# Ranking steps of the next expert head spread over two heads, and PSUM sums copied at once at a tile change

## The chip, the cores and the metric

One of the cores of a Trainium2 chip runs the whole program as one launch. Each core has five engines with queues of their own: PE (TensorE, matmuls into the accumulator memory PSUM), DVE (VectorE, elementwise work, reductions, top-8 searches), ACT (ScalarE, activation functions and copies), POOL (GpSimd, here the issuer of the indirect gathers) and SP (SyncE, here the issuer of plain transfers). 16 DMA engines move data between the large memory and SBUF. Engines meet through semaphores only. The metric is the device time of the program in microseconds, as the median of several runs. A difference of 0.2% of it is about the smallest that can be told from none.

## The reference

Two layers over 256 latent tokens (with a context of 256 tokens), model width 1024. Each layer is a mixer (a gated convolution with a gated DeltaNet in the first layer, multi-head latent attention in the second), followed by a channel mixer with product-key experts. The change touches the latter:

```python
def peer(h, w_q, sub_keys, u_tab, v_tab):      # P_BLOCK = 128 tokens, P_HEADS = 8, P_NKEYS = 128, P_TOPK = 16
    tok = h.reshape(-1, P_BLOCK, D)
    def one(hb):
        q = (hb @ w_q).reshape(P_BLOCK, P_HEADS, 2, P_DKEY // 2)
        s = jnp.einsum('thpk,hpnk->thpn', q, sub_keys).astype(jnp.float32)
        s1, i1 = lax.top_k(s[:, :, 0], P_TOPK)
        s2, i2 = lax.top_k(s[:, :, 1], P_TOPK)
        cand = (s1[..., :, None] + s2[..., None, :]).reshape(P_BLOCK, P_HEADS, P_TOPK * P_TOPK)
        sc, pos = lax.top_k(cand, P_TOPK)
        idx = (jnp.take_along_axis(i1, pos // P_TOPK, axis=-1) * P_NKEYS
               + jnp.take_along_axis(i2, pos % P_TOPK, axis=-1))
        gate = jax.nn.softmax(sc, axis=-1).astype(hb.dtype)
        act = jax.nn.gelu(jnp.einsum('td,thkd->thk', hb, u_tab[idx]), approximate=False)
        return jnp.einsum('thk,thkd->td', gate * act, v_tab[idx])
```

For each token and head two sets of 128 scores are cut to their 16 best, the 256 sums of pairs to the 16 best again, and those 16 experts' rows (a u row and a v row of 1024 numbers each) are fetched. The dot product of the token with u, through a gelu and times the gate, weighs v in the sum. The first layer does this for four tiles of 128 tokens (two of context, two of latents), the second for two.

## The kernel before

The program is a row of blocks; every engine has to reach the end of a block before any of them starts the next. The first block projects the inputs, runs the first layer's mixer for the context tiles (`mixer_dve(dve, 0)` and its fellows), and scores their experts. The second, `sums_and_mixer`, computes the expert sums of all four tiles of the first layer, 32 heads of a tile (G = 0 to 31), with the mixer of the other two tiles woven in. The third is the second layer's attention up to the scores. The last, `last_sums`, does the sums of two tiles (G = 32 to 47).

**One head.** A head has 16 experts per token, k = 0 to 15. POOL (`sums_pool`, L1255) gathers for each k one row pair per partition into one of eight ring slots of 8 KB per partition, as soon as `slot_free` tells that the slot is free again. DVE (`head_dve`, L1427) waits for the slot and forms the dot product of u with the tile's tokens. After every second k it tells ACT (`sums_act`), which computes gelu (L1270), the coefficient (L1271) and for each k a diagonal matrix of coefficients (L1275). PE (`head_pe`, L1342) multiplies diagonals and v rows, in a group of 16 matmuls of 64 rows and 512 columns for the two slots, adds them up in four PSUM banks, and frees both slots. So a head has eight pairs, j = 0 to 7.

**Sums.** Slots of a pair go to different halves of the partitions of PSUM: banks `sum_bank(i, c)` hold the sum of row half i of the tokens, once in the partitions of half i (the straight half) and once in those of the other (the crossed half). They are added at the end of a tile: ACT copies the crossed halves into the tile's place in `hx2` (`tile_sum_act`, L1311), DVE adds the straight ones to it (`tile_sum_dve`, L1317) and raises `peer_taken`. At the first head of the next tile PE waits for that (`tile_open_pe`, L1319) and clears all banks with 16 matmuls by zero (L1328); all the others add (`start=False`). Within a block DVE does this adding after its dot product k = `SUM_AT` = 3 of the next tile's first head.

**Ranking.** `rank_dve` is a generator of 16 steps, each ended by a wait for DVE's own instructions. It takes one head's 256 scores to expert numbers and gates: a copy of the scores (L1355), top-8 searches and replacements (L1360 to L1365) for both key sets, the 256 candidates (L1368), two rounds of top 8 among them (L1372 to L1381), positions split in two numbers (L1384, L1385), casts of uint32 to float32 (L1372, L1387), two one-hot masks times index tables and their reductions (L1390, L1394, L1398), then the expert numbers and gates (L1402 to L1406). While head G's dot products run, the ranking of head G+1 advances by two steps after each of k = 1 to 8 (`RANK_SLOTS`). ACT's exponential for its gates (`gate_exp_act`, L1281) is issued in the pair j = 2; it loads another activation table, and the next gelu loads its own again. The first head of a block has its ranking done in the block before it (`first_rank_dve`), between two copies of scores out of PSUM (L801 in the first layer, L1752 in the second).

**Mixer.** In `sums_and_mixer` each of ACT, PE and DVE calls `between()` at the pairs in `STAGE_AT` = (0, 4, 6), on DVE after k = 1, 9 and 13. A call runs the next stage of the mixer of the other two tiles, 46 stages in all, in the queue's order, waits included.

**Others.** `tile_start_dve` copies the tile's tokens to `hx_cur` (L1418). `peer_residual_dve` (L1461, L1464) multiplies a finished sum by its gate and adds it to the stream.

## Time and profile before

| | |
|---|---|
| Median of 3 runs | 2910.38 us (2910.12 to 2912.04) |
| The profiled execution | 2908.8 us |
| Its span, first to last instruction | 2907.0 us |
| Mean granted TensorE clock | 0.802 of full speed |
| Busy: PE, DVE, POOL, ACT | 1930.8, 1785.0, 971.5, 901.1 us |
| Mean rate of the DMA engines | 318 GB/s |

Each run's time is that of the whole program on the device; the span of the profile leaves out what lies before the first and after the last instruction. Busy times overlap, so they don't add up to the span. A row of a timeline gives the start in us, the duration in us, engine, line, operation, what it writes and reads, how many instructions are merged into the row, and in brackets how long the engine had been idle before, and what ended that idleness. `PEld` is PE's loading of weights, which runs beside its matmuls.

### The profile page before, as it was taken

How to read it: one execution, taken by the hardware profiler on the slowest of the kernel's cores; microseconds unless marked ns; L12 is line 12 of the kernel's file. 1: busy time of each engine (PE TensorE's matmuls, PEld its weight loads, DVE VectorE, ACT ScalarE, POOL GpSimd, SP SyncE). 2: the span in 40 equal slices, each digit the busy share in tenths (PEclk: the TensorE clock that was granted, in tenths of full speed). 3: DMA queues.
4: the chain of work that ended last, by engine and by line, in shares of the span. 5: the costliest groups of instructions: out<-in, count | busy, mean ns of one | idle time of the engine just before them, and what ended most of it. 6: DMA issues, size and time to landing. Idle time of an engine off the chain costs nothing. (4 is left out here: it accounts for less than half of the span.)

```text
span 2907.0 us, 31687 instructions
## 1 busy us (share of the span) xinstructions
PE 1930.8 (66%) x11320; PEld 836.7 (29%) x11320; DVE 1785.0 (61%) x4221; ACT 901.1 (31%) x2534; POOL 971.5 (33%) x897
## 2 busy tenths in 40 slices
PE   4999988666666666765555465566996555555564
PEld 2445885333332321331111111113455111111111
DVE  3044872787777774565777767764234677767774
ACT  1043111333333242332333333333221333333332
POOL 3000320344334432333444444450001444444542
PEclk7999998888778877886777777767998877777767
DMA  9112862799888998989999999993303999999997
GB/s 340 58 59 92 287 211 87 291 362 387 335 323 343 386 370 318 393 310 417 421 421 421 405 381 421 421 421 140 141 16 121 421 421 421 421 384 421 421 421 298
DMA packets 167551, 924.94 MB, mean 318 GB/s; under 512 B 17936, under 2 KB 20464, under 8 KB 67680
## 3 DMA queue, kind: packets, MB, share of 16 engines
q0 software_dynamic: 115056, 810.10, 68.5%
q1 hardware_dynamic: 51760, 110.70, 10.6%
q8 instruction: 90, 1.47, 0.2%
q10 hardware_dynamic: 576, 2.10, 0.2%
q14 instruction: 69, 0.57, 0.1%
HBM read 921.68 MB, written 1.15 MB: 317 GB/s over the span
## 5 line engine op out<-in xcount | busy, mean ns | idle before, releaser
L1342 PE MATMUL ps<-arena,diag 64*64 64x512 f32 x6144 | 1072.0, 832 | 815.1 <-ACT diag L1275 815.1
L1255 POOL DMA_INDIRECT arena<-in_experts,expert_cur x768 | 902.7, 1175 | 1463.5 <-PE ps L1342 1050.4
L1427 DVE CUSTOM_DVE_ANT_0 arena<-arena,hx_cur 128x1024 f32<-128x1024 f32 x768 | 937.4, 1227 | 493.5 <-DMA arena<-in_experts,expert_cur 474.9
L1342 PEld LDWEIGHTS ps<-arena,diag 64*64 64x64 f32 x6144 | 252.0, 169 | 1586.1 <-ACT diag L1275 1239.3
L1270 ACT ACTIVATE acts<-dots 128x2 f32<-128x2 f32 x384 | 78.1, 203 | 1212.9 <-DVE dots L1427 1212.2
L1275 ACT ACTIVATE diag<-consts,coef 128x128 f32<-128x128 f32 x768 | 266.1, 393 | 12.5
L1271 ACT ACTIVATE coef<-acts,gate_cur 128x1 f32<-128x1 f32 x768 | 184.8, 287 | 12.6
L1188 PE MATMUL ps<-arena,wring 128*128 128x512 f32 x384 | 168.8, 599 | 1.1 <-DVE arena L514 1.1
L983 POOL DMA_DIRECT2D mods<-hx_cur x48 | 26.7, 558 | 359.7 <-DVEq L978 354.1
L819 PE MATMUL ps<-arena 128*128 128x128 f32 x896 | 106.7, 277 | 2.7 <-issue 1.6
L819 PEld LDWEIGHTS ps<-arena 128*128 128x128 f32 x896 | 102.9, 192 | 6.4 <-DVE arena L672 3.3
L1188 PEld LDWEIGHTS ps<-arena,wring 128*128 128x128 f32 x384 | 73.8, 193 | 94.4 <-issue 94.4
L819 PEld LDWEIGHTS ps<-wring 128*128 128x128 f32 x640 | 83.3, 213 | 36.9 <-issue 36.9
L819 PE MATMUL ps<-wring 128*128 128x128 f32 x640 | 88.7, 300 | 0.0
L963 PE MATMUL ps<-wring,small 128*2 128x128 f32 x1536 | 57.7, 314 | 33.9 <-DMA wring<-in_w_mod 33.9
L1764 PE MATMUL ps<-wring,arena 128*128 128x512 f32 (+2 forms) x204 | 77.8, 544 | 1.8 <-DVE arena L514 1.1
L1270 ACT ACT_TABLE_LOAD x52 | 66.7, 1283 | 19.7 <-DVE dots L1427 18.8
L1427 DVE DVE_READ_ACCUMULATOR2_ANT dots<- 128x1 f32 x768 | 63.2, 82 | 0.0
L1281 ACT ACT_TABLE_LOAD x48 | 61.6, 1283 | 0.9
L897 PE MATMUL ps<-wring,arena 128*128 128x512 f32 x128 | 58.6, 616 | 0.0
L972 DVE TENSOR_TENSOR hx_cur<-ps,hx_cur 2x128 f32<-2x128 f32 x96 | 27.4, 285 | 47.5 <-PE ps L963 46.3
L963 PEld LDWEIGHTS ps<-wring,small 128*2 128x2 f32 x1536 | 42.3, 96 | 45.8 <-DMA wring<-in_w_mod 26.4
(253 smaller groups left out, 1822.0 us busy)
## 6 DMA issues: line engine op xcount, KB each, us to landing
wring<-in_w_mod SPq DMA_DIRECT2D x24, 2048.0 KB, 9.0
wring<-in_ev_w_in SPq DMA_DIRECT2D x7, 2048.0 KB, 7.7
wring<-in_p_w_q SPq DMA_DIRECT2D x6, 2048.0 KB, 9.4
arena<-in_experts,expert_cur POOLq DMA_INDIRECT x768, 11.5
wring<-in_ev_w_out SPq DMA_DIRECT2D x4, 2048.0 KB, 16.9
wring<-in_od_w_out SPq DMA_DIRECT2D x2, 2048.0 KB, 8.0
arena<-mods SPq DMA_DIRECT2D x3, 1024.0 KB, 36.8
wring<-mods SPq DMA_DIRECT2D x5, 512.0 KB, 9.2
```

What stands on the lines that cost most here:

```text
L819: last = M(dst, lhsT(h), rhs(h), start=True, stop=True) if op is M else TR(dst, lhsT(h), rhs(h))
L897: last = M(bank, y, w[:, k, :], start=(k == 0), stop=(k == KT - 1))
L963: last = nc.tensor.matmul(ps[32 * g:32 * g + 2, 6 + n % 2, 0:P], sT[:, 2 * k:2 * k + 2], w[:, k, g, :], start=(k == 0), stop=(k == KT - 1))
L1188: last = M(dst, l, r, start=(i == 0), stop=(i == len(pairs) - 1))
L1255: nc.gpsimd.indirect_dma_start(ring[:, k % RING, :], None, table, bass.IndirectOffsetOnAxis(ap=expert_cur[:, par, k:k + 1], axis=0),).then ...
L1270: act_step(nc.scalar.activation(acts[:, par, g], dots[:, par, g], ACT.Gelu))
L1271: act_step(*[nc.scalar.activation(coef[:, par, k:k + 1], acts[:, par, k:k + 1], ACT.Copy, scale=gate_cur[:, par, k:k + 1]) for k in range( ...
L1275: nc.scalar.activation(diag[:, k % RING, :], const(IDENT), ACT.Copy, scale=coef[:, par, k:k + 1]).then_inc(diag_ready, 1)
L1281: nc.scalar.activation(gate_exp[:, :], best[:, :], ACT.Exp, bias=gate_stat[:, 0:1], accum_out=gate_stat[:, 1:2]).then_inc(gexp_ready, 1)
L1342: last = nc.tensor.matmul(ps[rows_of(o), sum_bank(i, c), :], diag[rows_of(i), slot, rows_of(i)], ring[rows_of(i), slot, D + 512 * c:D + 51 ...
L1427: ins = nc.vector.tensor_tensor_reduce(out=ring[:, slot, 0:D], in0=ring[:, slot, 0:D], in1=hx_cur[:, :], scale=1.0, scalar=0.0, op0=ALU.mu ...
L1764: last = M(dst, l, r, start=(i == 0), stop=(i == len(pairs) - 1))
```

## The change

The ranking has 14 steps. The first copy is gone, the searches read the scores where they lie; both casts are gone, and the mask, multiplication and reduction take uint32 operands directly, each as one instruction over both key sets (512 elements a partition). The ranking of head G+1 takes one step after each of k = 9 to 15 of head G-1 (seven steps), and one after each of k = 0 to 6 of head G (seven). Before the first head of a block, the whole ranking of its first head and seven steps of its second run. ACT's exponential is issued in the pair j = 1. The dot products read the tile's tokens in `hx2` without a copy. At the change of tile DVE copies the straight halves to `straight` after k = 3, PE waits for these and ACT's two copies only, DVE adds afterwards, and the zero matmuls are gone: the first group of a tile writes with `start=True`. Nothing is computed otherwise.

```diff
         def tile_sum_act(act, T_, place):
 
-            act.wait_ge(slot_free, (T_ + 1) * SLOTS + RING)
-            total = place.rearrange("p (a b) -> p a b", a=2)
+            tile_summed(act, T_)
             for i in range(2):
-                nc.scalar.copy(total[rows_of(i)], sum_of(i, 1 - i)).then_inc(crossed, 1)
+                nc.scalar.copy(place.rearrange("p (a b) -> p a b", a=2)[rows_of(i)], sum_of(i, 1 - i)).then_inc(
+                    peer_crossed, 1)
 
         def tile_sum_dve(dve, T_, place):
 
-            dve.wait_ge(crossed, 2 * T_ + 2)
-            total = place.rearrange("p (a b) -> p a b", a=2)
-            dve_step(*[nc.vector.tensor_tensor(total[rows_of(i)], sum_of(i, i), total[rows_of(i)], ALU.add)
-                       for i in range(2)])
-            dve.sem_inc(peer_taken, 1)
+            tile_summed(dve, T_)
+            for i in range(2):
+                nc.vector.tensor_copy(straight.rearrange("p (a b) -> p a b", a=2)[rows_of(i)], sum_of(i, i)).then_inc(
+                    peer_straight, 1)
+            dve.wait_ge(peer_straight, 2 * T_ + 2)
+            dve.wait_ge(peer_crossed, 2 * T_ + 2)
+            dve_step(nc.vector.tensor_tensor(place, place, straight[:, :], ALU.add))
 
         def tile_open_pe(pe, T_):
 
-            pe.wait_ge(peer_taken, T_ + 1)
-            sum_banks_taken(pe)
-            for c in range(2):
-                for i in range(2):
-                    for o in range(2):
-                        nc.tensor.matmul(ps[rows_of(o), sum_bank(i, c), :], const(ZERO)[rows_of(i), 0:HALF],
-                                         consts[rows_of(i), 0:512], start=True, stop=True)
+            if T_ == 0:
+                sum_banks_taken(pe)
+            else:
+                pe.wait_ge(peer_crossed, 2 * T_)
+                pe.wait_ge(peer_straight, 2 * T_)
...
-                                                    start=False, stop=True, skip_group_check=True)
+                                                    start=opens, stop=True, skip_group_check=True)
...
-            step(V.tensor_copy(score_cur[:, :], arena[:, n * 256 + 16384:n * 256 + 16640]))
-            yield
...
-            step(V.tensor_copy(top_idx_f[:, :, :], top_idx[:, :, :]), V.max(best[:, 0:8], cand[:, :]))
+            step(V.max(best[:, 0:8], cand[:, :]))
...
-            step(V.tensor_copy(pos_ab_f[:, :, :], pos_ab[:, :, :]))
-            yield
-            hot = (onehot, cand)
-            step(*[V.tensor_tensor(square(hot[i]), iota16[:, :].unsqueeze(1).broadcast_to((P, TOPK, TOPK)),
-                                   pos_ab_f[:, i, :].unsqueeze(2).broadcast_to((P, TOPK, TOPK)), ALU.is_equal)
-                   for i in range(2)])
-            yield
...
+            step(V.tensor_tensor(onehot[:, :, :, :], iota16[:, :].unsqueeze(1).unsqueeze(1).broadcast_to(across),
+                                 pos_ab[:, :, :].unsqueeze(3).broadcast_to(across), ALU.is_equal))
+            yield
+            step(V.tensor_tensor(onehot[:, :, :, :], onehot[:, :, :, :],
+                                 top_idx[:, :, :].unsqueeze(2).broadcast_to(across), ALU.mult))
+            yield
+            step(V.tensor_reduce(sel_ab[:, :, :], onehot[:, :, :, :], AX, ALU.add))
...
-        RANK_SLOTS = range(1, 9)
+        RANK_FROM = 9
+        RANK_EARLY = TOPK - RANK_FROM
+        RANK_STEPS = 14
...
                 if k == SUM_AT:
                     sum_before()
-                if rank_next and k in RANK_SLOTS:
-                    next(rank)
-                    next(rank)
+                if rank_next is not None and k < RANK_STEPS - RANK_EARLY:
+                    next(rank_next)
+                if rank_after is not None and k >= RANK_FROM:
+                    next(rank_after)
...
-        def first_rank_dve(G, n):
-
-            for _ in rank_dve(G, n, 0):
-                pass
+        def first_ranks_dve(ranks):
+
+            rank_steps(ranks[0], 0, RANK_STEPS)
+            rank_steps(ranks[1], 0, RANK_EARLY)
```

## Rows read from the trace of the kernel before

**Rows 1.** The page: DMA queue of the gathers, and two of the costliest groups

```profile
q0 software_dynamic: 115056, 810.10, 68.5%
...
L1427 DVE CUSTOM_DVE_ANT_0 arena<-arena,hx_cur 128x1024 f32<-128x1024 f32 x768 | 937.4, 1227 | 493.5 <-DMA arena<-in_experts,expert_cur 474.9
...
L1281 ACT ACT_TABLE_LOAD x48 | 61.6, 1283 | 0.9
```

**Rows 2.** Busy time by stretch: woven stretch, a full one, two woven heads

```profile
core 0: us, PE busy (x) PEld busy (x) DVE busy (x) ACT busy (x) POOL busy (x), PEclk, DMA share, GB/s
529.90:1280.50 750.60, 488.02 (x2992) 228.09 (x2992) 526.91 (x1263) 250.62 (x740) 278.40 (x240) 0.80 0.90 354
1345.00:1655.00 310.00, 177.29 (x989) 40.41 (x980) 212.38 (x538) 107.78 (x338) 148.75 (x126) 0.74 1.01 421
...
582.50:623.10 40.60, 27.46 (x188) 14.09 (x192) 31.60 (x80) 17.34 (x53) 17.16 (x14) 0.84 0.88 344
710.80:765.20 54.40, 36.22 (x240) 17.42 (x240) 39.42 (x89) 15.04 (x47) 18.69 (x18) 0.78 0.90 344
```

**Rows 3.** Waits (us, times, longest): two of 529.9 to 1280.5, one of the span

```profile
POOL arena L1255 <- PE ps L1342: 417.8, 98, 18.6
...
DVE arena L1427 <- DMA arena<-in_experts,expert_cur: 70.6, 50, 5.9
...
PE ps L1328 <- DVEq L1319: 38.7, 4, 10.7
```

**Rows 4.** Groups of instructions on DVE, shapes apart (busy us, mean ns)

```profile
L1355 DVE COPY score_cur<-arena 128x256 f32<-128x256 f32 x48 | 13.9, 289 | 0.0
...
L672 DVE TENSOR_TENSOR wring<-wring,consts 128x512 f32<-128x512 f32 x24 | 15.5, 689 | 1.5
...
L1387 DVE CAST pos_ab_f<-pos_ab 128x32 f32<-128x32 uint32 x48 | 8.6, 178 | 0.1
```

**Rows 5.** Timeline of the tile change from 2567 to 2582 us

```profile
2567.82 2.04 ACT L1311 COPY arena<-ps 64x1024 f32<-64x1024 f32 x2 [3.45 <-PE ps L1342]
...
2573.14 2.47 DVE L1317 TENSOR_TENSOR arena<-ps,arena 64x1024 f32<-64x1024 f32 x2
...
2575.72 3.29 PE L1328 MATMUL ps<-consts 64*64 64x512 f32 x16 [7.95 <-DVEq L1319]
...
2578.84 3.60 PE L1342 MATMUL ps<-arena,diag 64*64 64x512 f32 x32
...
2581.04 1.05 POOL L1255 DMA_INDIRECT arena<-in_experts,expert_cur  x1 [9.86 <-PE ps L1342]
```

**Rows 6.** Timeline of the first ranking, up to the first gather

```profile
510.00 0.49 DVE L1360 MAX8 top_val<-score_cur 128x8 f32<-128x128 f32 x2
...
515.28 0.09 DVE L1381 MATCH_VALUE_LOAD best_pos<-best,cand_left 128x8 f32 x1
...
516.32 0.43 DVE L1390 TENSOR_TENSOR onehot<-iota,pos_ab_f 128x256 f32<-128x256 f32 x1
516.66 0.42 DVE L1390 TENSOR_TENSOR cand<-iota,pos_ab_f 128x256 f32<-128x256 f32 x1
...
520.97 0.18 DVE L1402 SCALAR_TENSOR_TENSOR expert_cur<-sel_ab 128x16 uint32<-128x16 f32 x1 [2.32 <-ACT gate_exp L1281]
...
524.05 1.01 POOL L1255 DMA_INDIRECT arena<-in_experts,expert_cur  x1 [94.30 <-issue]
```

**Rows 7.** Timeline, dot products on DVE: the first, and k = 2 and 9 of a head

```profile
529.88 1.23 DVE L1427 CUSTOM_DVE_ANT_0 arena<-arena,hx_cur 128x1024 f32<-128x1024 f32 x1 [5.94 <-DMA arena<-in_experts,expert_cur]
...
723.14 1.23 DVE L1427 CUSTOM_DVE_ANT_0 arena<-arena,hx_cur 128x1024 f32<-128x1024 f32 x1
...
740.25 1.23 DVE L1427 CUSTOM_DVE_ANT_0 arena<-arena,hx_cur 128x1024 f32<-128x1024 f32 x1 [0.19 <-DVE gate_cur L1406]
```

**Rows 8.** Timeline of the end of the first layer's sums

```profile
1986.60 2.04 ACT L1311 COPY arena<-ps 64x1024 f32<-64x1024 f32 x2 [2.97 <-PE ps L1342]
1988.67 2.48 DVE L1317 TENSOR_TENSOR arena<-ps,arena 64x1024 f32<-64x1024 f32 x2 [6.52 <-ACT arena L1311]
1991.37 1.23 DVE L1461 TENSOR_TENSOR arena<-arena,wring 128x1024 f32<-128x1024 f32 x1 [0.22 <-DVEq L1319]
```

More of the change, by code:

```diff
@@ L169, in build @@
         conv_w = sb("conv_w", [P, 16, 3])
-        hx_cur = sb("hx_cur", [P, D])
-        score_cur = sb("score_cur", [P, 2 * NKEY])
+        straight = sb("straight", [P, D])
         score_left = sb("score_left", [P, 2 * NKEY])
@@ L211, in area @@
                                **{k: s for k, s in zip(names[:-1], shape)})
-        mod_row = [hx_cur[:, P * k:P * k + P] for k in range(4)]
+        mod_row = [straight[:, P * k:P * k + P] for k in range(4)]
         norm_row = [diag[:, k, :] for k in range(4)]
@@ L1290, in head_act @@
                 sums_act(act, G, par, j)
-                if j == 2 and rank_next:
+                if j == 1 and rank_next:
                     gate_exp_act(act, G + 1)
@@ L1334, in head_pe @@
                     between()
-                if j == 0 and G % PH == 0:
+                opens = j == 0 and G % PH == 0
+                if opens:
                     tile_open_pe(pe, G // PH)
@@ L1408, in rank_dve, with rank_steps, head_dve @@
             yield
-        RANK_SLOTS = range(1, 9)
+        RANK_FROM = 9
+        RANK_EARLY = TOPK - RANK_FROM
+        RANK_STEPS = 14
         STAGE_AT = (0, 4, 6)
         SUM_AT = 3
-        def tile_start_dve(T_, place):
-            if T_:
-                dve_step.eng.wait_ge(dots_ready, T_ * (PH * GROUPS_OF_HEAD))
-            dve_step(nc.vector.tensor_copy(hx_cur[:, :], place))
-        def head_dve(dve, G, n, par, rank_next, between=lambda: None, sum_before=lambda: None):
-            rank = rank_dve(G + 1, n + 1, 1 - par)
+        RANKS = [rank_dve(G, G % (4 * PH), G % 2) for G in range(6 * PH)]
+        def rank_steps(rank, first, last):
+            for _ in range(first, last):
+                next(rank)
+        def head_dve(dve, G, place, rank_next, rank_after, between=lambda: None, sum_before=lambda: None):
             for k in range(TOPK):
@@ L1427, in head_dve @@
                 ins = nc.vector.tensor_tensor_reduce(
-                    out=ring[:, slot, 0:D], in0=ring[:, slot, 0:D], in1=hx_cur[:, :], scale=1.0, scalar=0.0,
-                    op0=ALU.mult, op1=ALU.add, accum_out=dots[:, par, k:k + 1])
+                    out=ring[:, slot, 0:D], in0=ring[:, slot, 0:D], in1=place, scale=1.0, scalar=0.0,
+                    op0=ALU.mult, op1=ALU.add, accum_out=dots[:, G % 2, k:k + 1])
                 if k % GRP == GRP - 1:
@@ L1435, in head_dve, with heads_dve @@
                     sum_before()
-                if rank_next and k in RANK_SLOTS:
-                    next(rank)
-                    next(rank)
+                if rank_next is not None and k < RANK_STEPS - RANK_EARLY:
+                    next(rank_next)
+                if rank_after is not None and k >= RANK_FROM:
+                    next(rank_after)
+        def heads_dve(dve, heads, T0, between=lambda: None, at_head=lambda G: None):
+            first, end = heads[0], heads[-1] + 1
+            ranks = {G: RANKS[G] for G in heads}
+            for G in heads:
+                t = G // PH - T0
+                at_head(G)
+                head_dve(dve, G, tile_place(t), ranks.get(G + 1), ranks.get(G + 2), between,
+                         (lambda: tile_sum_dve(dve, G // PH - 1, tile_place(t - 1))) if t and G % PH == 0
+                         else (lambda: None))
+            tile_sum_dve(dve, end // PH - 1, tile_place(t))
         def tile_place(i):
             return hx2[:, i, :]
-        def first_rank_dve(G, n):
-            for _ in rank_dve(G, n, 0):
-                pass
+        def first_ranks_dve(ranks):
+            rank_steps(ranks[0], 0, RANK_STEPS)
+            rank_steps(ranks[1], 0, RANK_EARLY)
         def peer_gate_dma(sp, layer):
@@ L1507, in _, with at_head @@
                 between = weave(mixer_dve(dve, 1))
-                def sum_before(t):
-                    return lambda: tile_sum_dve(dve, t - 1, tile_place(t - 1))
-                for G in range(4 * PH):
-                    t = G // PH
+                def at_head(G):
                     if G == 3 * PH:
@@ L1518, in _ @@
                         peer_residual_dve(dve, 0, 2)
-                    if G % PH == 0:
-                        tile_start_dve(t, tile_place(t))
-                    head_dve(dve, G, G, G % 2, G < 4 * PH - 1, between,
-                             sum_before(t) if t and G % PH == 0 else lambda: None)
-                tile_sum_dve(dve, 3, tile_place(3))
+                heads_dve(dve, range(4 * PH), 0, between, at_head)
                 peer_residual_dve(dve, 0, 3)
@@ L1549, in _, with at_head @@
             def _(dve):
-                for G in range(G0, 6 * PH):
+                def at_head(G):
                     if G == 6 * PH - 2:
                         peer_residual_dve(dve, 1, 2)
-                    if G % PH == 0:
-                        tile_start_dve(G // PH, tile_place(G // PH - T0))
-                    head_dve(dve, G, G - G0, G % 2, G < 6 * PH - 1, sum_before=(
-                        lambda: tile_sum_dve(dve, T0, tile_place(0))) if G == 5 * PH else lambda: None)
-                tile_sum_dve(dve, T0 + 1, tile_place(1))
+                heads_dve(dve, range(G0, 6 * PH), T0, at_head=at_head)
                 peer_residual_dve(dve, 1, 3)
```

29 lines of the change are left out of this document (12 added, 17 removed).

## The prediction, made blind

> **What bounds the kernel now.** I read four views in this order.
>
> First the groups of instructions on the page. 768 gathers move 810 MB, 1.055 MB each, and every one is followed by one dot product on DVE of 1.23 us [rows 1].
>
> Then the busy time by stretch. From 1345 to 1655 us the DMA engines are full (share 1.01) at 421 GB/s [rows 2]. At that rate a gather needs 1.055/421 = 2.5 us and a head of 16 gathers 40.1 us. There no work taken from DVE, ACT or PE is worth anything. The same holds for the second layer's sums. Only the first stretch, 529.9 to 1280.5, is different: 354 GB/s, share 0.90. It runs from the first dot product to that of the 16th head: 15 heads (240 gathers issued) in 750.6 us, 50.0 us a head against the floor of 40.1. There the layer's mixer is woven in between the dot products, three stages a head (after k = 1, 9 and 13). Two heads show the spread: one of 40.6 us, at the floor, and one of 54.4 us [rows 2].
>
> Then who waits in that stretch. POOL waits 417.8 us for PE to free a ring slot, and DVE waits only 70.6 us for gathers [rows 3]. So DVE, where dot products, ranking and mixer stages queue up, paces most of these heads. In the 54.4 us head the dots of k = 2 to k = 9 start 17.1 us apart in all, with seven dots of 1.23 us in it: 8.5 us is ranking steps, back to back, while gathers have already landed [rows 7].
>
> Last the order of time around a tile change. PE's sum banks are copied out, and PE can't go on until DVE has reached its fourth dot product and added. Then 16 zero matmuls run for 3.3 us before the first real group starts at 2578.84, and POOL, idle 9.86 us, issues again at 2581.04 [rows 5]. Four of the six tiles have such a change (38.7 us of PE's wait in 4 of them [rows 3]); the two that open a layer hide theirs under the first gather.
>
> **The change, part by part.** The sum is made against the profiled execution, 2908.8 us (span 2907.0); the median of the runs shown is 2910.4, so 1.6 is added at the end.
>
> *Work that leaves DVE's queue.* Per head: the score copy 0.29, one cast hidden behind the next instruction (0.1 of its 0.18) and one on its own (0.18 and the step's wait, 0.2) [rows 4]. Three pairs of 256 elements become three single instructions of 512. A pair takes 0.34 + 0.43 = 0.77 because the second starts 0.34 after the first [rows 6]; the nearest 512-element row is 0.69 [rows 4]. That is 0.08 each, 0.25 together. Sum 0.85, with two steps' waits fewer about 1.0 us a head. The uint32 operands of the new instructions have no row of this size; the casts read uint32 at no visible penalty, so I take none, and bound it at one pair's price, that is a loss of the 0.25. In the two full stretches this is worth 0, because DMA hides it. In the woven heads it is worth 1.0 x 16 = 16 us where DVE paces. Against the row stands the Trainium skill, VectorE: DVE Perf Modes, section "The TRN2 errata": SBUF sources pay a fixed latency per instruction, (N+151)/0.96 ns. By it each merged pair would save 157 ns, not 80, and the woven heads some 4 us more. The row of the pair shows most of that latency already overlapped, so the row decides.
>
> *Ranking moved.* 14 steps instead of 16: seven in k = 9 to 15 of the head before (5.2 us, from 510.00 to 515.28 less the hidden cast [rows 6]) and seven in k = 0 to 6 (about 3.6 us: 0.5, 0.35, three times 0.69, 0.35, 0.3). Before, all 9.7 us lay in k = 1 to 8. So the half-head k = 1 to 8 loses about 6.6 us and k = 9 to 0 gains 5.7. In a head with both halves paced by DVE, as the 54.4 us one, the two cancel but for the 1.0 above. A half that is at the floor of 20 us gives nothing back when made lighter. Bounds for the woven part besides the 16: another 15 us gained, a fifth of DVE's 70.6 us of waits [rows 3], since a smoother queue keeps gathers in flight; or all the 16 lost. I take -16, the removed work alone.
>
> *Exp moved.* ACT's exponential with its two table loads of 1.28 us [rows 1] goes from pair j = 2 to j = 1. DVE needs it after k = 5 now, before after k = 8. At the floor's pace that is 5 us after k = 3, enough. With dots back to back it is 2.4 + 1.4 us, just about ACT's work. I take 0; the one row of such a wait is 2.32 us [rows 6], the bound for a DVE-paced head. `ranked` comes two slots earlier; POOL does not wait for it now, so 0.
>
> *Tile start.* The copy into hx_cur goes, 0.69 us six times, hidden under landing gathers except where DVE is late; the dot products read SBUF in both versions, 0.
>
> *Tile change.* DVE now copies its two halves out of PSUM, and PE waits only for the copies. The nearest rows for 64x1024 out of PSUM are 1.22 us (DVE's add) and 1.0 (ACT's copy) [rows 5]; I take 1.2, so DVE's two take 2.4, as the adds do. The zero matmuls go: -3.3 us. But they ran from a cold start, after 7.95 us of PE idleness, 3.3 us for 16, which is the 1.2 GHz level, and left the clock up for the group behind them (3.6 us for 32, the 2.4 GHz level) [rows 5]. Without them the first real group of 16 runs cold: 3.5 us instead of 1.8. The gain at the first freed slot is 3.3 - 1.7 + 0.4 (DVE late by 0.4 at its fourth dot because of the ranking) = 2.0 us. Where DVE is late by a mixer stage or a residual (two of four changes), lighter steps at k = 1 and 2 (1.0 instead of 2.4) and the missing copy add up to 2 us more. Sum 2 x 2.0 + 2 x 3.5 = -11; ends -5 and -18. DVE's extra add of 1.22 us lies after the copies, takes up what the removed copies give, and delays the fifth dot by nothing. The skill's page TensorE: Matmul & The Clock Gate, Part 1, says that the array starts at half rate after idleness, and this trace agrees; a count that ignored it would have put the four changes at -18.
>
> *Stage ends.* After the last group ACT copies for 2.04 us, then DVE adds for 2.48, and the residual starts at 1991.37 [rows 8]. Now DVE copies beside ACT from 1986.6 to 1989.0 and adds for 1.22: 1990.4. Twice -0.9 = -1.8.
>
> *Stage starts.* This is the price. The first ranking now also runs seven steps of the second head before DVE takes the last scores out of PSUM and reaches the block's end; POOL's first gather waits for that end (524.05) [rows 6]. Nothing covers it: +5.2 in the first layer, where the first ranking ends by ACT's exponential anyway (wait 2.32), and +4.5 in the second, where the shorter first ranking gives 0.6 back. Together +9.7.
>
> Sum: -16 - 11 - 1.8 + 9.7 = -19, so 2889.7 profiled, and 2891.3 as a median.
>
> **The rivals.**
> (A) The forecast, -19.
> (B) The spread pays beyond the work removed: gathers stay in flight through the stages and DVE's waits shrink by a fifth. -34, 2876. For it: the long runs of ranking after each first stage. Against: heads such as the 40.6 us one are at the floor already.
> (C) The woven heads are paced by PE and ACT around the stages, not by DVE's sum, so the 16 is lost: -3, 2907. For it: in the stages DVE itself waits for PE's mixer matmuls.
> (D) Slower. The seven early steps fall into k = 9 to 15, where two of the three stages lie. By the starts of the 256 dot products of the woven heads, from 529.88 on [rows 7], DVE waits for no or hardly any gather in that half in seven of the 16, so each pays 5.7 us, 40 together. The lighter first halves give back at most 31 in those heads (to the floor of 20), and only about half if the ring has run dry by then; the other heads give some 13. Woven +12, total +9, 2919. It decides where a second half grows past about 28 us: then the gathers in flight, eight slots of 2.5 us and a way through ACT and PE, no longer bridge it.
> (E) The merged instructions don't get cheaper, or a uint32 operand is dear. Up to 5 us of A, no case of its own.
> That the change doesn't do what it says I can exclude by the code: the steps, copies and zero matmuls are gone from every head and tile.
>
> **How the numbers follow.** Chances: A 0.50, B 0.20, C 0.16, D 0.14. The predicted time is A's, 2891. A's own range is 2880 to 2902 (tile changes -5 to -18, woven part -8 to -22). The range takes in B's and C's times with some of the bounds on B's side: 2868 to 2911. It leaves out D and the tail beyond B. A difference under 0.2%, 5.8 us, can't be told from none. Faster holds A, B and a quarter of C (0.74); the same the rest of C and a little of D (0.14); slower D (0.12).
>
> **What would show each step.** The first 15 heads should take about 736 us instead of 750.6, at some 361 GB/s, and stay 421 in the full stretches. DVE's starts from k = 2 to 9 should take 12 to 14 us in a heavy head instead of 17.1, and those of k = 10 to 15 should grow by 4 to 5. At a tile change PE's first real group should start about 2.4 us after DVE's fourth dot and take 3.5 us for its 16, and POOL's idle time should be 7.5 to 8 us, not 9.86. The first gather should be issued at about 529.2. The forecast is wrong if the woven heads' mean stays at 50 us or more (C, D), if DVE shows waits for ACT's exponential in the woven heads, or if the first gather is not later.

## The result: no gain, and what the profile after shows

The changed kernel takes 2916.6 us, the median of 20 runs (2909.8 to 2929.7), against 2909.2 of the kernel before in 20 runs beside them: ratio 1.0027, 95% interval 1.0018 to 1.0036, that is 7.9 us slower. Run again later, on the chip of the first experiments below, it took 2907.6 against 2908.4 there: 0.9999, interval 0.9986 to 1.0012. So it is nowhere faster, and at most some 0.3% slower. Forecast were 2891 us and a ratio of .993. The profiled execution took 2916.25 us, its span is 2914.4.

The work did leave DVE. Its busy time fell from 1785.0 to 1731.5 us, and the merged instructions cost what was forecast. These are groups of instructions on DVE after, shapes apart (busy us, mean ns, idle before):

```profile
L1386 DVE TENSOR_TENSOR onehot<-onehot,top_idx 128x512 f32<-128x512 f32 x48 | 33.0, 687 | 0.2
L1383 DVE TENSOR_TENSOR onehot<-iota,pos_ab 128x512 f32<-128x512 f32 x48 | 32.9, 686 | 0.1
L1389 DVE TENSOR_REDUCE sel_ab<-onehot 128x32 f32<-128x512 f32 x48 | 32.7, 681 | 0.1
L1317 DVE COPY straight<-ps 64x1024 f32<-64x1024 f32 x12 | 14.6, 1220 | 9.5 <-PE ps L1343 9.3
L1321 DVE TENSOR_TENSOR arena<-arena,straight 128x1024 f32<-128x1024 f32 x6 | 7.3, 1224 | 0.2
```

A uint32 operand costs nothing extra (.686 against the .689 that I took from a float row [rows 4]), so rival E did not come about. DVE copies 64x1024 out of PSUM in 1.22 us. The pair took .77 us and the merged instruction takes .686, so the measured saving is .08. By the fixed latency per instruction that the Trainium skill gives (VectorE: DVE Perf Modes, section "The TRN2 errata") a merged pair would save an estimated 157 ns. Two instructions in a row on DVE overlap here (the second starts .34 us after the first), and the measured number decides.

But what DVE no longer works it now waits. The dot products' group on the page after:

```profile
L1419 DVE CUSTOM_DVE_ANT_0 arena<-arena 128x1024 f32<-128x1024 f32 x768 | 941.7, 1227 | 565.9 <-DMA arena<-in_experts,expert_cur 553.2
```

553.2 us of waits for gathers stand where 474.9 stood [rows 1]. The first 15 heads took as long as before, 750.2 us against 750.6 [rows 2], while the full stretch stayed full (busy time by stretch, after):

```profile
core 0: us, PE busy (x) PEld busy (x) DVE busy (x) ACT busy (x) POOL busy (x), PEclk, DMA share, GB/s
537.50:1287.70 750.20, 484.93 (x2976) 226.06 (x2976) 514.24 (x1172) 252.50 (x743) 277.11 (x241) 0.80 0.90 355
1345.00:1655.00 310.00, 174.49 (x992) 40.77 (x992) 203.99 (x504) 105.80 (x332) 149.36 (x122) 0.76 1.01 420
```

The waits of that stretch, after. POOL's stands beside 417.8 and DVE's beside 70.6 before [rows 3]; ACT's exponential now holds DVE up four times, the longest 1.9 us:

```profile
POOL arena L1251 <- PE ps L1343: 426.5, 93, 12.7
...
DVE arena L1419 <- DMA arena<-in_experts,expert_cur: 83.4, 64, 6.7
...
DVE expert_cur L1392 <- ACT gate_exp L1277: 5.2, 4, 1.9
```

The starts cost what was forecast. The timeline of the first layer's: the first ranking ends by the exponential's wait, seven steps of the second head follow from 524.24 on, and the first gather goes out at 531.84.

```profile
523.58 0.17 DVE L1392 SCALAR_TENSOR_TENSOR expert_cur<-sel_ab 128x16 uint32<-128x16 f32 x1 [3.16 <-ACT gate_exp L1277]
...
524.24 0.49 DVE L1358 MAX8 top_val<-arena 128x8 f32<-128x128 f32 x2
...
531.84 1.00 POOL L1251 DMA_INDIRECT arena<-in_experts,expert_cur  x1 [99.67 <-issue]
```

The last score copy ahead of the ranking stands at 511.67 us here and at 509.07 before (nothing changed ahead of them), so the way to the first gather grew from 15.0 to 20.2 us: +5.2. In the second layer the time from the last copies of the first layer's sums to the first gather grew from 245.9 to 250.7: +4.8.

### The profile page after: what moved, and what is told of

Read it like the earlier page. It is cut to its first block and busy times, and to the rows that moved or that the text cites. A ratio compares the mean times of both kernels' runs of the same rounds, so it can differ in the third digit from the quotient of the medians.

```text
span 2914.4 us, 31460 instructions
## 1 busy us (share of the span) xinstructions
PE 1911.9 (66%) x11224; PEld 834.7 (29%) x11224; DVE 1731.5 (59%) x3933; ACT 905.3 (31%) x2534; POOL 995.7 (34%) x897
## 5 line engine op out<-in xcount | busy, mean ns | idle before, releaser
L1251 POOL DMA_INDIRECT arena<-in_experts,expert_cur x768 | 926.9, 1207 | 1448.8 <-PE ps L1343 1017.8
L1419 DVE CUSTOM_DVE_ANT_0 arena<-arena 128x1024 f32<-128x1024 f32 x768 | 941.7, 1227 | 565.9 <-DMA arena<-in_experts,expert_cur 553.2
L1271 ACT ACTIVATE diag<-consts,coef 128x128 f32<-128x128 f32 x768 | 267.6, 395 | 12.4
L980 POOL DMA_DIRECT2D mods<-straight x48 | 26.7, 558 | 362.5 <-DVEq L975 356.9
L969 DVE TENSOR_TENSOR straight<-ps,straight 2x128 f32<-2x128 f32 x96 | 27.4, 286 | 48.2 <-PE ps L960 46.7
## 6 DMA issues: line engine op xcount, KB each, us to landing
wring<-in_ev_w_out SPq DMA_DIRECT2D x4, 2048.0 KB, 12.8
```

What stands on the lines that cost most here:

```text
L1251: nc.gpsimd.indirect_dma_start(ring[:, k % RING, :], None, table, bass.IndirectOffsetOnAxis(ap=expert_cur[:, par, k:k + 1], axis=0),).then ...
L1271: nc.scalar.activation(diag[:, k % RING, :], const(IDENT), ACT.Copy, scale=coef[:, par, k:k + 1]).then_inc(diag_ready, 1)
L1419: ins = nc.vector.tensor_tensor_reduce(out=ring[:, slot, 0:D], in0=ring[:, slot, 0:D], in1=place, scale=1.0, scalar=0.0, op0=ALU.mult, op1 ...
```

## Experiments

All compare with runs of the kernel before on the same chip (medians of 2907.3 to 2908.6). Two chips took part: the first eight rows behind the first comparison, down to the load in S, ran on one, the other seven on the other. Across the two the ratios are the safer measure; differences of medians are given too, and the kernel before differs by 1.3 us at most between these runs. With the few runs of each kernel a difference of two of these ratios is uncertain by some .002 to .003, 6 to 9 us. Beside the ratio I use **woven**, the time of the first 15 heads from the first dot product to that of head 15, and its two halves, **F** (from the dot of k = 1 to that of k = 9, summed over the 15 heads) and **S** (from k = 9 to k = 1 of the next head). These come from one profile each, and the same kernel can differ: the changed kernel has woven 750.2 in its first profile and 733.0 in its second. Its two halves differ by 14 and by 3 us. So a difference of some 15 us in woven or F says nothing by itself.

| kernel | median us | ratio, 95% interval | woven | F | S |
|---|---|---|---|---|---|
| before | | 1 | 750.6 | 382.8 | 365.6 |
| changed, first time | 2916.6 | 1.0027, 1.0018 to 1.0036 | 750.2 | 333.8 | 414.6 |
| changed, again | 2907.6 | .9999, .9986 to 1.0012 | 733.0 | 319.5 | 411.4 |
| tile change only | 2903.2 | .9977, .9962 to .9991 | 739.2 | 380.4 | 356.5 |
| lighter steps, old slots | 2898.5 | .9969, .9955 to .9984 | 746.5 | 365.6 | 378.5 |
| lead inside | 2895.3 | .9960, .9945 to .9975 | 737.8 | 326.4 | 409.8 |
| banks taken at k = 1 | 2897.7 | .9957, .9940 to .9975 | 742.9 | 323.5 | 417.2 |
| lead and banks | 2888.7 | .9937, .9922 to .9952 | 748.3 | 325.9 | 421.0 |
| load in F | 2951.8 | 1.0161, 1.0141 to 1.0180 | 791.2 | 425.8 | 363.3 |
| load in S | 2926.9 | 1.0079, 1.0060 to 1.0098 | 763.5 | 382.3 | 379.2 |
| load under cover | 2914.9 | 1.0020, 1.0004 to 1.0036 | 750.5 | 417.8 | 330.7 |
| late steps covered | 2881.8 | .9911, .9897 to .9925 | 735.7 | 330.2 | 403.2 |
| early steps covered | 2865.9 | .9860, .9841 to .9880 | 716.5 | 322.1 | 392.6 |
| both covered | **2849.6** | **.9798, .9770 to .9826** | 708.4 | 331.9 | 374.2 |
| both, in the changed kernel | 2866.5 | .9856, .9841 to .9871 | 716.0 | 338.4 | 375.2 |
| one block | 2967.4 | 1.0194, 1.0163 to 1.0225 | 738.1 | 415.0 | 320.6 |
| PE kept busy | 2917.5 | 1.0032, 1.0016 to 1.0048 | 744.8 | 330.4 | 412.6 |

### The change taken apart

**Tile change only**: the kernel before with the new copies, no zero matmuls and no copy into `hx_cur`; its ranking as it was.

> The kernel before with the new tile change alone (straight halves copied by DVE, PE released by the copies, no zero matmuls, dot products on the tokens in place); ranking and its slots as before. Theory A (zero matmuls off the path, but the first groups cold): 4 to 7 us faster than before, POOL idle about 8.2 us at the change where it was 9.9. Theory B (my forecast's terms): 12 us faster. Theory C (the cold groups and DVE's extra add give all of it back): within 2 us.

**Lighter steps, old slots**: the changed kernel with all 14 steps two a slot, as before.

```diff
-                if rank_next is not None and k < RANK_STEPS - RANK_EARLY:
-                    next(rank_next)
-                if rank_after is not None and k >= RANK_FROM:
-                    next(rank_after)
+                if rank_next is not None and k in RANK_SLOTS:   # range(1, 8)
+                    next(rank_next)
+                    next(rank_next)
```

> The change with its 14 lighter steps put back into the old slots: two steps after each of k = 1 to 7 of the head before, the exponential at j = 2, no ranking ahead of a block. It keeps the lighter steps and the new tile change. Theory 1 (the spread eats what the lighter steps give in the woven heads, and the ranking ahead costs 9.7 us at the two starts): 11 to 20 us faster than before, and the first 15 woven heads take 736 to 745 us. Theory 2 (DVE's queue does not pace the woven heads, lighter steps are worth nothing): about 4 to 6 us faster than before, from the tile change and ends alone, and those heads stay at 750. Theory 3 (the lighter steps or the new tile change are themselves slow): no faster than before.

**Lead inside**: the changed kernel, the early steps of a block's second head run in the block, behind the first gathers.

```diff
-            rank_steps(ranks[1], 0, RANK_EARLY)
...
             ranks = {G: RANKS[G] for G in heads}
+            rank_steps(RANKS[first + 1], 0, RANK_EARLY)
```

> The change, but the seven early steps of a block's second head run after the block has begun, while the first gathers are on their way, and not before its start. Theory 1: 9.7 us less than the changed kernel, so 1 to 3 us faster than before; the first gather follows the first scores' copy by 15 us in the first layer as before, not 20. Rival (the starts only shift work that is hidden elsewhere): as the changed kernel, some 8 us slower than before.

**Banks taken at k = 1**: the changed kernel with `SUM_AT = 1`.

> The changed kernel with DVE's copies after k = 1 instead of k = 3 of the next tile. Theory A (PE's wait for DVE's turn sets the hole in the gathers): PE goes on 4 to 5 us earlier at the changes in the full stretches, the hole of about 4 us in the DMA stream closes there, 6 to 14 us less than the changed kernel over four changes. Theory B (the hole is set by PE's cold groups and POOL's issue pace): at most 3 us less. Theory C: DVE, queued behind the end of PE's last group, holds back its dot products and the time rises.

The new tile change alone gives 6.7 us (2.6 to 11). Put beside it, the lighter steps in the old slots give only 2.3 more by the ratios (4.7 by the medians), where 16 were forecast. In the halves F fell by 15 against the tile change only, 1.0 us a head as I had counted, and S grew by 22. Those are one profile each and hardly clear of what two profiles of one kernel differ by; the spreading shows the same on a larger scale. In the six kernels that spread the steps one a dot, F is 320 to 334 and S 410 to 421; in the three that leave them where they were, 366 to 383 and 357 to 379. What the spreading takes from F, 50 us on the mean, comes back in S, 48 us. The lead inside starts the gathers 15.0 us after the score copies again, not 20.2.

**Changed, again**, and **lead and banks** (both edits together), to see them side by side on one chip.

> The changed kernel again, on the same chip as the three below, so that they can be compared with it directly. If its ratio to the kernel before (1.003 measured) belongs to the kernel, it comes out at 1.000 to 1.005 here too, and the kernels measured against before at .996 are really 15 us or more ahead of it. If that ratio came from that chip or those runs, it comes out at .997 to .999, and the early steps of the second head cost no more than the 5 us a stage start that the traces show.

> Both starts mended (the seven early steps of the second head run behind the first gathers) and the banks taken after the second dot product of a tile, not the fourth. If the parts add: 10 us from the two starts, 3 to 6 us from the four tile changes, against the changed kernel: 13 to 16 us under it, ratio to before about .994. If the gathers make good by the next stage what is won at a start or a tile change, it is no faster than the kernels with one of the two, .996.

The changed kernel comes out level with the one before, and 18.9 us behind the two edits together. They are worth what was expected of them, a little more (13 to 16). Their woven stretch is no shorter. So neither the starts nor the tile changes explain the missing 16 us.

### Where does DVE's queue count?

Three kernels add the same load to the kernel before, in each of the first 16 heads, four pairs of instructions that write where nothing reads:

```diff
+                if G < 2 * PH and k in (2, 3, 5, 6):        # second kernel: (10, 11, 12, 14)
+                    dve_step(nc.vector.tensor_tensor(scratch[:, 0:256], consts[:, 0:256], consts[:, 0:256], ALU.mult),
+                             nc.vector.tensor_tensor(scratch[:, 256:512], consts[:, 0:256], consts[:, 0:256], ALU.add))
```

> The kernel before with 8 more products or sums of 256 elements on DVE in each of the first 16 heads, two each after k = 2, 3, 5 and 6; nothing reads them. By my rows they are about 2.8 to 3.1 us a head, 45 to 50 us together. My prediction's theory, DVE's queue paces these heads, says at least 40 us more. Rival C, the rest of a stage paces them, says under 10. A ring that runs dry in some halves and bridges the others says 15 to 35.

> The same 8 instructions in each of the first 16 heads, two each after k = 10, 11, 12 and 14, the half in which the changed kernel put the seven early steps. If DVE's queue paces these halves, 40 us or more, and the spreading then has to cost in them what it saves in the first halves. If this half has slack that its stages leave, under 15. Rival D (second halves dear, first halves with less to give back) says that this one costs more than the same load in the first halves, by 10 us or more.

DVE's busy time in the woven stretch rose by 45.7 us in the first and 44.3 in the second, 3 us a head. After k = 2, 3, 5 and 6 nearly all of it is paid: +43 us by the medians, 47 by the ratio (41 to 52). After k = 10, 11, 12 and 14 about half: +18 by the medians, 23 by the ratio (17 to 29). Rival D, for which the second halves are the dear ones, said otherwise, and so did rival C. It led to a new theory. A stage stands in PE's queue two dots earlier than in DVE's: PE takes it before group j, and DVE after the *second* dot of pair j. By this theory two of the four places of the load in S, k = 11 and 12, are free, and none of those in F. The head of [rows 7] shows it, before:

```profile
735.68 1.22 DVE L1427 CUSTOM_DVE_ANT_0 arena<-arena,hx_cur 128x1024 f32<-128x1024 f32 x1
...
738.61 3.66 PE L1342 MATMUL ps<-arena,diag 64*64 64x512 f32 x16 [1.84 <-ACT diag L1275]
742.20 2.05 PE L819 MATMUL ps<-wring 128*128 128x128 f32 x16
744.09 3.74 PE L819 MATMUL ps<-arena 128*128 128x128 f32 x32
...
745.18 0.69 DVE L713 TENSOR_TENSOR wring<-ps,small 128x512 f32<-128x512 f32 x1 [3.70 <-PE ps L819]
```

The dot of k = 7 starts at 735.68. From it hang ACT's coefficients, PE's group (738.61), the stage's matmuls (742.20) and with them DVE's next instruction of the stage at 745.18, 9.50 us later. In that time DVE has four ranking steps (2.3 us) and the dots of k = 8 and 9, and still waits 3.70 us. After, no step stands there, and the same head shows:

```profile
744.95 1.29 DVE L1419 CUSTOM_DVE_ANT_0 arena<-arena 128x1024 f32<-128x1024 f32 x1 [0.18 <-DVE gate_cur L1396]
...
747.31 1.21 DVE L1419 CUSTOM_DVE_ANT_0 arena<-arena 128x1024 f32<-128x1024 f32 x1
...
754.21 1.29 DVE L710 TENSOR_TENSOR wring<-ps,small 128x512 f32<-128x512 f32 x2 [5.67 <-PE ps L816]
```

k = 9 comes 2.36 us after k = 7, not 4.57 [rows 7], and the stage 9.26 us after k = 7, not 9.50: the wait grew to 5.67. The two heads differ in more than the steps: PE's group took 1.95 us here and 3.66 before, and the stage's row on DVE stands 4.56 us behind its first matmul (749.65) here and 2.98 before. A cleaner test adds work and changes nothing else. So the third kernel puts the load there, two pairs after k = 7 and two after k = 8.

> The kernel before with the same 8 extra instructions in each of the first 16 heads (2.8 to 3.1 us a head, 45 to 48 together), four after k = 7 and four after k = 8. New theory: the stage that DVE takes up after k = 9 needs matmuls that stand on PE behind the group of k = 6 and 7, so from the dot of k = 7 on, DVE's own work up to the stage is covered by ACT's coefficients (1.9 us), PE's group (1.95) and the stage's matmuls (up to 7). By it this load costs 0 to 15 us, where the same load after k = 2, 3, 5 and 6 cost 43. If only DVE's sum counts, it costs 40 or more here too.

The load is nearly free there: +6 us (1 to 10) where it cost 43. Its rows in the same head:

```profile
737.70 1.23 DVE L1428 CUSTOM_DVE_ANT_0 arena<-arena,hx_cur 128x1024 f32<-128x1024 f32 x1
...
745.40 1.22 DVE L1428 CUSTOM_DVE_ANT_0 arena<-arena,hx_cur 128x1024 f32<-128x1024 f32 x1
...
747.32 0.69 DVE L714 TENSOR_TENSOR wring<-ps,small 128x512 f32<-128x512 f32 x1 [0.68 <-PE ps L820]
```

k = 9 comes 7.70 us after k = 7 and the stage still 9.62 us after k = 7. The wait has shrunk to 0.68: the cover is used up. Three more heads show it, by the same rows: from the dot of k = 7 to the stage behind k = 9 it is 9.66 us before and 9.67 with the load in the first head, 12.15 and 12.16 in the 13th, 15.44 and 15.45 in the 15th.

This is not the whole of it. In ten of the 15 heads DVE does not wait for PE behind k = 9 at all, before and with the load. What the load filled over the 15 heads, 3.05 us in each, are DVE's waits for PE at that stage (24.4 us before, 11.5 with the load), its waits for gathers at k = 8 to 10 (19.3 and 3.0), and later waits for gathers, at k = 11 to 14 (26.4 and 15.4). So PE's answer hides a part of it, and gathers that are still on their way the larger part. What the two are worth apart was not tested.

### Steps put under cover

**Both covered**: lead and banks as above, with other places for the steps.

```diff
-                if rank_next is not None and k < RANK_STEPS - RANK_EARLY:
-                    next(rank_next)
-                if rank_after is not None and k >= RANK_FROM:
-                    next(rank_after)
+                for _ in range(LATE_AT.get(k, 0) if rank_next is not None else 0):      # {7: 4, 8: 3}
+                    next(rank_next)
+                for _ in range(EARLY_AT.get(k, 0) if rank_after is not None else 0):    # {11: 3, 12: 3, 15: 1}
+                    next(rank_after)
```

> The last combination (lead inside, banks taken after the second dot product) with the ranking steps put where by the new theory a stage's matmuls cover them: the early seven three after k = 11, three after k = 12, one after k = 15, the late seven four after k = 7 and three after k = 8. The theory says that the first 15 heads take 700 to 725 us, where the spread ones took 733 to 750, and the whole 15 to 40 us less than the last combination: 2850 to 2875, ratio .980 to .989. If DVE's sum paces these heads, wherever the steps stand, no change: .994.

2849.6 us, 39 less than the same kernel with the steps one a dot (40 by the ratios), and 59 less than the kernel before. The woven heads move 376 GB/s at a share of .94, where they moved 354 at .90 [rows 2]; in the full stretch nothing changed. Busy time by stretch:

```profile
534.50:1242.80 708.30, 484.08 (x2976) 227.87 (x2976) 517.25 (x1172) 250.90 (x743) 280.39 (x241) 0.82 0.94 376
1345.00:1600.00 255.00, 143.82 (x816) 34.81 (x816) 174.50 (x415) 89.82 (x279) 119.18 (x101) 0.75 1.01 420
```

Then each half alone, and both in the changed kernel with its starts and its tile change as they are.

> The last combination (2888.7, ratio .9937) with only the seven late steps moved, four after k = 7 and three after k = 8; the early ones stay one a dot in k = 9 to 15. By the cover theory the late steps of k = 1 to 6, 3.1 us, stand ahead of the dot of k = 7 that the stage's matmuls wait for; in the ten or so heads with a heavy stage there, this gives 15 to 30 us of the 39 that both moves gave: ratio .984 to .989. If the early steps are what costs, .993.

> The same with only the seven early steps moved, three after k = 11, three after k = 12, one after k = 15. By the theory some 3 of their 5.2 us stood uncovered in k = 9, 10, 13 and 14; moved, they give 10 to 25 us: ratio .985 to .990. If the two moves add, this one and the one before it give 39 us together; if the stage's wait in a half is one and the same for both, they give less each than their share, or one gives all.

> The changed kernel, its starts, tile change and copies as they are, only the 14 steps' places as in the kernel at ratio .980. If the slots alone are the cause, it comes out 35 to 45 us under the changed kernel (ratio .9999 to 1.0027 to before): .985 to .989. If they help only together with the other two edits, above .992.

The late steps alone give 7 us, less than I had expected; the early ones alone give 23, both 39. So the seven early steps, one a dot from k = 9 on, were the dearer half, as rival D had it. That both give 9 more than the sum of the two is within the noise of four ratios.

The waits say what the steps filled, over 15 heads, against the kernel with lead and banks. At the stage after k = 13, where the early steps stand in front, DVE's waits for PE fell from 42.5 to 14.0 us: PE's answer covers them. At the stage after k = 9 they fell from 27.5 to 24.3 only. There the late steps filled waits for gathers, 47.6 to 14.1 at k = 8 to 10, and the like came up where they had stood, 8.6 to 46.4 at k = 3 to 7. This fits the small gain of the late steps.

In the changed kernel itself the places alone give 41 us: it then beats the kernel before by 1.4%.

**One block**: the lighter steps of one head in k = 7 and 8 alone, seven each, no spreading over heads, the exponential in pair j = 3, banks taken at k = 1.

> No spreading at all: the 14 lighter steps of the next head in two blocks of seven, 5.2 us after k = 7 and 3.6 us after k = 8 in the same head, the exponential in pair j = 3, banks taken after the second dot product. By the theory 8.8 us plus two dots is a little more than what the lighter stages cover, and the other two stages' halves stay as light as before the spreading: the first 15 heads at 705 to 730 us, ratio .982 to .991. If a block of 9 us delays the coefficients of k = 8 and 9 and so the slots in every head, it is slower than the kernel before.

The woven stretch is 738.1, not 705 to 730, and the whole 56 us slower than the kernel before by the ratio. The loss is in the full stretches, which leave the floor (busy time by stretch):

```profile
1345.00:1655.00 310.00, 153.72 (x912) 38.49 (x912) 199.08 (x487) 101.27 (x314) 125.79 (x115) 0.73 0.95 389
```

389 GB/s where it was 421 [rows 2]; a head takes 43 us there, not 40.1. My reading is that without a stage nothing covers a run of 9 us, and a ring of eight slots does not bridge it, as it does the 5.2 us of the kernel above. This kernel differs in more than the run, and no run takes it apart; ACT's wait for the ranking with its exponential in j = 3 (18.3 us in 8 heads) does not look like the cause, as ACT then is idle for another 4.63 us before DVE's next pair of dots is done (the head at 1430 us).

### PE's clock at a tile change

**PE kept busy**: lead inside, and at two tile changes zeros multiplied into a free bank right behind the last group.

```diff
+                if T_ in (3, 5):
+                    for _ in range(24):
+                        nc.tensor.matmul(ps[:, 0, :], const(ZERO), consts[:, 0:512], start=True, stop=True)
                 pe.wait_ge(peer_crossed, 2 * T_)
```

> The changed kernel with the lead inside, and 24 matmuls of zeros of 512 columns into a bank that is free by then, on PE right behind the last group of a tile, at the changes into tiles 3 and 5 (head 24 and head 40). If PE's clock after its idle time is what makes the first group slow, as I read it, the first 16 matmuls of the new tile take 1.8 to 2.0 us at the 2.4 GHz level and not 3.5, and POOL issues 2 to 3 us earlier. The total moves by 5 us at the most, less than these rounds resolve. If it is the order of the copies and not the clock, the group takes 3.5 us here too.

PE's timeline at the first of the two:

```profile
1656.59 20.87 PE L1330 MATMUL ps<-consts 128*128 128x512 f32 x48
1677.39 7.10 PE L1346 MATMUL ps<-arena,diag 64*64 64x512 f32 x64
```

The reading of the clock holds: behind matmuls the new tile's groups take 7.10 us for 64, 1.78 for 16, the 2.4 GHz level; behind 7.39 us of idle time they took 7.19 for 33 (the rows of the tile change below), 3.5 for 16, the 1.2 GHz level. The Trainium skill (TensorE: Matmul & The Clock Gate, Part 1) says that the array runs at half rate after idleness, and this trace agrees. But I had sized the zeros wrong by four: 24 of them are 48 matmul records of .43 us, 20.9 us in all, and POOL was idle for 19.09 us instead of 8. Two such changes cost the kernel about 21 us by the ratios against the one with the lead inside. That a shorter run of zeros would pay was not tried.

## Why the prediction was wrong

**Work that leaves DVE's queue (-16 us): wrong, the step that failed.** Its size was about right: DVE's busy time in the 15 heads fell from 526.9 to 514.2 us [rows 2]. Its premise, that DVE's sum paces the woven heads wherever the work stands, was not. Counting DVE's waits for gathers [rows 3] told me that gathers were in time, not that DVE's queue was the bound. I left out its waits for PE inside the stages, 118 us in all. The three largest, before, in the view and stretch of [rows 3]:

```profile
DVE arena L801 <- PE ps L923: 31.5, 3, 11.9
DVE wring L521 <- PE ps L897: 27.7, 3, 11.0
DVE wring L735 <- PE ps L819: 27.6, 28, 4.8
```

The lighter steps also came to stand differently. The mean distances between dots over the 15 heads, us:

| from dot to dot | before | changed | changed, again | both covered |
|---|---|---|---|---|
| k = 1 to 7 | 19.9 | 17.5 | 16.4 | 15.7 |
| 7 to 10 | 11.2 | 11.7 | 11.4 | 12.4 |
| 10 to 14 | 14.2 | 14.9 | 15.1 | 14.5 |
| 14 to next 1 | 4.6 | 5.8 | 5.8 | 4.5 |

From 7 to 10 nothing came of 2.3 us of steps taken away (0.5 came in behind the stage, and the distance grew by as much). Waits took their place, for gathers above all: 19.3 us over the 15 heads before, 43.5 after, and those for PE at the stage went from 24.4 to 30.4. From 10 to 14 0.7 is paid of some 3.3 us of early steps put there, from 14 to 1 1.2 of some 1.9. From 1 to 7 some 4.3 us of ranking went (9.7 less the 2.3 before, 3.6 less 0.5 after) and 2.4 came of it in the first profile, 3.5 in the second. Of the rest in the first, 28 us over the 15 heads, waits for gathers at k = 2 to 7 took 12 (1.3 before, 12.9 after), those for PE at the stage after k = 1 took 9 (38.3 and 47.6) and the exponential 5. That the place in the queue decides is shown by the loads and by the kernels that differ in the places alone. That it decides through PE's place is shown where the stage waits for PE, in the heads read above and at the stage after k = 13; elsewhere the slack is in the gathers.

**The rivals.** D named what happened: the second halves grew by 49 us (I had put 40), the first gave 49 back (31 and 13). Its net was close, 0 where I had 12. Its reason, the ring running dry, is borne out in part: DVE's waits for gathers grew from 18.0 to 48.5 us in F and fell from 44.6 to 26.4 in S. But uncovered work is as dear in F: the load there costs more than the one in S, of which half stands under cover. C, the removed 16 us lost, was right in its result, and its reason, PE's matmuls in the stages, was right for the way from k = 7 to the stage and wrong for k = 1 to 7, where added work is paid in full. Both cases had 0.30 together; A had 0.50. B did not come about with this placement; with another it did, and more.

**Stage starts (+9.7): right.** +5.2 and +4.8. Nothing covered them.

**Tile change (-11) and stage ends (-1.8): right in sign, 6.7 us for both where 12.8 were forecast**, interval 2.6 to 11. At the change that I had read:

```profile
2578.12 2.04 ACT L1310 COPY arena<-ps 64x1024 f32<-64x1024 f32 x2 [3.62 <-PE ps L1343]
...
2581.72 1.23 DVE L1419 CUSTOM_DVE_ANT_0 arena<-arena 128x1024 f32<-128x1024 f32 x1 [0.65 <-DMA arena<-in_experts,expert_cur]
2582.87 2.47 DVE L1317 COPY straight<-ps 64x1024 f32<-64x1024 f32 x2
...
2585.44 7.19 PE L1343 MATMUL ps<-arena,diag 64*64 64x512 f32 x33 [7.39 <-DVE straight L1317]
...
2589.42 1.84 POOL L1251 DMA_INDIRECT arena<-in_experts,expert_cur  x1 [8.16 <-PE ps L1343]
```

POOL's idle time is 8.16 us, not 9.86 [rows 5]: -1.7, forecast -2.0. PE's groups run cold, 3.5 us for 16, as worked out, but the second one too (33 matmuls in 7.19 us), which I had not counted; behind the zeros the second ran at the full clock [rows 5]. From ACT's copies at the end of the second tile to those of the fourth the time fell by 1.1 us, in the second layer from the first gather to the last copies by 1.7, with one quiet change in each (2.0 forecast; in its second profile by 2.7 and 2.9). The two changes in woven heads can't be told from the noise of those heads. At the end of the first layer the copies run side by side and the residual starts 3.76 us after ACT's copies, not 4.77 [rows 8]: -1.0 (-0.9):

```profile
1991.96 2.04 ACT L1310 COPY arena<-ps 64x1024 f32<-64x1024 f32 x2 [2.62 <-PE ps L1343]
1991.96 2.47 DVE L1317 COPY straight<-ps 64x1024 f32<-64x1024 f32 x2 [4.11 <-PE ps L1343]
1994.47 1.22 DVE L1321 TENSOR_TENSOR arena<-arena,straight 128x1024 f32<-128x1024 f32 x1
1995.72 1.22 DVE L1466 TENSOR_TENSOR arena<-arena,wring 128x1024 f32<-128x1024 f32 x1
```

**Exp moved (0): nearly right**, 5.2 us of waits in 15 heads, 11.0 in the second profile. The prediction had named such waits as a sign of being wrong.

**The signs in the dots.** In the heavy head of [rows 7] the dots of k = 2 to 9 start 10.96 us apart, not 12 to 14, where it was 17.1, and those of k = 10 to 15 grew by 2.2, from 13.4 to 15.6, not by 4 to 5. Over all 16 heads the first stretch shrank by 3.0 us on the mean (18.2 to 15.2) and the second grew by 1.2 (15.7 to 16.9).

**The sum** by what was measured: 10.0 for the starts, -6.7 for tile changes and ends, and for the ranking what is left. The changed kernel stands 6 to 15 us over the one with the tile change only, 10 of it the starts: the ranking is worth -4 to +5, where -16 was forecast. Why the changed kernel lost 7.9 us in its first runs and none in the later ones is open.

## What to carry to other kernels

Where one engine's queue mixes own work with stages that wait for another engine, ask of every piece of work what waits behind it on the *other* engine. Work ahead of the last input that the other engine needs is paid in full; work between that input and the wait for the answer is free up to the length of the answer, or fills waits for transfers that stand there. Here the same 3 us a head cost 43, 18 or 6 us by place alone, and moving steps without changing them gave 39 us, more than the 16 us of work that the change had removed from the woven heads. A step spread evenly is cheap only where it fills such a wait; and the kernel with one run of 9 us lost its time in the stretches without stages.

## What the runs showed that was not expected

A matmul of zeros with 128x128 weights and 512 float32 columns takes .43 us a record, where the groups' matmuls with 64x64 weights come to .11 each (7.10 us for 64 right behind them): nearly a factor of four, so one can't be priced from the other. DVE reads uint32 next to float32 without a penalty. And one execution's woven stretch can differ from another's by 17 us for the same kernel (750.2 and 733.0), with a granted clock of .80 and .82 in it.
